# A long single-core transformer kernel: all matmuls whose result nobody reads are removed

## What is computed

```
h = x
n = rms_norm(h, ln_mix_g);  proj = n @ w_in
ya = dilated_mixture(qa, ka, va) @ w_branch_a          # softmax attention in windows, 3 dilations
yb = stick_breaking(qb, kb, vb) @ w_branch_b           # sweeps over 128-key blocks, backwards
h = h + (gate_a * ya + gate_b * yb) @ w_out
n = rms_norm(h, ln_x_g);    h = h + memory_cross_attn(n, rms_norm(mem, ln_mem_g), ...)
n = rms_norm(h, ln_ffn_g);  h = h + conv_gated_mlp(n, w_up, conv_w, conv_b, w_down)
h = rms_norm(h, ln_f_g)
# second block
p = rms_norm(h, norm_pre) @ w_in2
fox = softmax attention with a decay bias, 8 heads     # in 4 pairs of heads
mla = latent attention, 8 heads                        # in 4 pairs of heads
out = h + rms_norm([fox, mla] @ w_out2, norm_post)
```

## Time and profile before

| | |
|---|---|
| median of 3 executions | 3004.85 us (3004.74 to 3006.88) |
| profiled execution, its own time | 3007.79 us |
| its span, first to last instruction | 3006.0 us |
| TensorE busy (matmul) | 2886.6 us, 96% |
| VectorE / ScalarE / GpSimd busy | 1485.9 / 950.1 / 788.4 us |
| mean granted TensorE clock | 0.986 of full speed |

### The profile page before, as it was taken

The page is one execution under the profiler, slowest core; times in us unless marked ns, Lnnn a source line. Parts: engine busy times, 40 slices in busy tenths (PEclk is TensorE's granted clock), DMA queues, the critical chain, the costliest instruction groups (busy, mean ns, idle before and its releaser), DMA issues.

```text
span 3006.0 us, 36445 instructions
## 1 busy us (share of the span) xinstructions
PE 2886.6 (96%) x13664; PEld 2249.3 (75%) x13664; DVE 1485.9 (49%) x1765; ACT 950.1 (32%) x1536; POOL 788.4 (26%) x514
## 2 busy tenths in 40 slices
PE   6999999999999999999999999999999999999998
PEld 5888785566577777677888888887787777877766
DVE  7464565644543335444433444433426655377764
ACT  4322226655600003232221221112214444254441
POOL 5312202322233331103332233232121011231225
PEclk8999999999999999999999999999999999999999
DMA  6200100000111110101111111111201001000023
GB/s 211 71 22 29 36 15 8 22 22 19 63 46 45 48 44 28 36 15 49 49 42 49 49 49 42 49 49 42 84 23 29 22 22 26 11 7 6 15 99 119
DMA packets 166342, 128.62 MB, mean 43 GB/s; under 512 B 19264, under 2 KB 150048, under 8 KB 165968
## 3 DMA queue, kind: packets, MB, share of 16 engines
q1 hardware_dynamic: 164816, 118.55, 13.0%
q10 hardware_dynamic: 1408, 8.50, 0.7%
HBM read 114.20 MB, written 12.65 MB: 42 GB/s over the span
## 4 chain that ended last, share of the span: by engine, by line
PE 64%; DVE 6%; ACT 1%; issue 1%; DMA 1%; POOL 0%; SPq 0%; DVEq 0%; ACTq 0%; POOLq 0%
PE ps L723 17%; PE ps L725 16%; PE ps L724 16%; PE ps L2825 2%; PE ps L2665 2%; PE ps L636 2%; PE ps L2720 1%; PE ps L2921 1%; PE ps L2721 1%; PE ps L2722 1%; PE ps L2922 1%; PE ps L2923 1%; DVE max_parts L2291 1%; DVE dF L2236 1%; PE ps L2897 1%
## 5 line engine op out<-in xcount | busy, mean ns | idle before, releaser
L723 PE MATMUL ps<-NH,w_high 128*128 128x512 f32 (+2 forms) x1992 | 772.3, 388 | 14.1 <-POOL w_low L1070 8.0
L724 PE MATMUL ps<-NL,w_high 128*128 128x512 f32 (+2 forms) x1992 | 772.9, 388 | 0.0
L725 PE MATMUL ps<-NH,w_low 128*128 128x512 f32 (+2 forms) x1992 | 770.1, 387 | 0.0
L1068 POOL CAST w_high<-w_raw 128x1024 fp32r<-128x1024 f32 x193 | 208.0, 1078 | 1931.8 <-PE ps L725 1147.0
L1070 POOL TENSOR_TENSOR w_low<-w_raw,w_high 128x1024 fp32r<-128x1024 f32 x193 | 480.8, 2491 | 15.4
L723 PEld LDWEIGHTS ps<-NH,w_high 128*128 128x128 f32 x1992 | 376.8, 189 | 101.8 <-issue 11.0
L724 PEld LDWEIGHTS ps<-NL,w_high 128*128 128x128 f32 x1992 | 376.6, 189 | 77.5
L725 PEld LDWEIGHTS ps<-NH,w_low 128*128 128x128 f32 x1992 | 376.9, 189 | 76.9
L819 DVE TENSOR_TENSOR hT<-hT,ps 128x1024 f32<-128x1024 f32 x168 | 205.1, 1221 | 250.2 <-PE ps L725 250.2
L723 PE MATMUL ps<-act_high,w_high 128*128 128x512 f32 x352 | 141.3, 401 | 2.9 <-DVE act_low L1968 2.9
L725 PE MATMUL ps<-act_high,w_low 128*128 128x512 f32 x352 | 139.4, 396 | 0.0
(11 more groups left out here) (406 smaller groups left out, 5279.5 us busy)
## 6 DMA issues: line engine op xcount, KB each, us to landing
w_raw<-in_w_in SPq DMA_DIRECT2D x69, 512.0 KB, 3.8
w_raw<-in_w_up SPq DMA_DIRECT2D x44, 512.0 KB, 3.8
w_raw<-in_w_out SPq DMA_DIRECT2D x24, 512.0 KB, 3.5
w_raw<-in_w_down SPq DMA_DIRECT2D x22, 512.0 KB, 3.8
w_raw<-in_w_xkv SPq DMA_DIRECT2D x8, 512.0 KB, 5.6
x_in<-in_x SPq DMA_DIRECT2D x8, 512.0 KB, 9.1
residual_spill<-hT SPq DMA_DIRECT2D x1, 4096.0 KB, 13.6
hT<-residual_spill ACTq DMA_DIRECT2D x1, 4096.0 KB, 13.0
```

What stands on the lines that cost most here:

```text
L723: nc.tensor.matmul(o, wh, xh, start=start, stop=False)
L724: nc.tensor.matmul(o, wh, xl, start=False, stop=False)
L725: return nc.tensor.matmul(o, wl, xh, start=False, stop=stop)
L1068: nc.gpsimd.tensor_copy(WH[slot][:, :], w_raw[slot][:, :]).then_inc(w_high, 1)
```

## The change

`busy` and all its calls are taken out. Nothing else differs: no wait, buffer, order or size. The argument `rows_gap` of `attend_pe` stays and is no longer used.

```
         def norm_pe(pe, name, first=0):
...
             norm_rows(pe, name)
-            if name in UPDATED:
-                busy(bank[1], 14)
...
-        def busy(o, n):
-
-            for _ in range(n):
-                nc.tensor.matmul(o, identb, masks[:, 0:4, :].rearrange("p a b -> p (a b)"), start=True, stop=True)
...
                         b = bank[A.bank(unit)]
-                        if (h, g, u) == (0, 0, 0):
-                            busy(b, 11)
                         pe.wait_ge(a_row, 2 * p + h + 1)
...
                             products(n - 2)
-                        if n == 0:
-                            wait_bank(pe, SB, i, U + 3)
-                            busy(bank[SB.bank(U + 3)], 8)
                         if n < 24:
                             sums(n)
...
-            busy(bank[0], 28)
             pe.wait_ge(g_m, G.iters + 2)
...
-            busy(bank[0], 32)
             pe.wait_ge(f_lo, FFN.iters * 2 + 4)
...
                         wait_bank(pe, st, i, U + unit)
-                        if n == 0:
-                            busy(bank[st.bank(U + unit)], rows_gap)
                         pe.wait_ge(p_rows[h], pb * 32 + 32)
...
             wait_bank(pe, MLA, 0, 0)
-            busy(bank[MLA.bank(0)], 20)
...
                 wait_bank(pe, OUT, 0, u)
-            busy(bank[0], 6)
             for g in range(2):
```

## The result

The changed kernel takes 3038.14 us (median of 4, 3034.67 to 3040.79); the kernel before, run beside it, 3005.77 us (median of 4). The ratio is 1.0106, 95% interval 1.0092 to 1.0119: 1.1% slower, 32 us. I had forecast 3024 us with a range of 3013 to 3034. The direction was right, the size was not: the measured time lies above the range.

The account below looks back on a forecast made before the run. TensorE, busy for 96% of the span, was taken to bound the kernel. Falls of its clock at the emptied waits, 3.4 + 4.0 + 2.0 + 6.0 + 0.3 + 1.6 + 1.4 = 18.7 us, on 3004.85 gave 3024 us, range 3013 to 3034.

Parts of the forecast that it names:

- end of `G`: One wait of 7.30 us at the end of loop `G`: the clock falls, costing 2.0 us.
- `FFN`: One wait of 9.90 us at the loop's end: the clock falls already, 1.70 us are paid, so only 0.3 more.
- the norms: Three waits of 3.80 us in norms `x`, `ffn`, `fin`: nothing hides a fall, 2.0 us each, 6.0 together.
- rival 4: The extra matmuls do not hold the clock, which falls anyway; time 3005 us; chance 0.03.
- rival 3: In the norms, `G` and `A` the engine feeding TensorE is slower and covers the slow stretch; 3003.8 us; chance 0.05.
- rival 1: Short waits, the four of `SB` and four of `FOX`, cost nothing; time 3018 us; chance 0.20.
- `SB`: Four waits of 2.30 us ahead of the sweeps: eight in ten fall at 1.25 us each, 4.0 together; bounds 0 and 13.6.
- `MLA`: One wait of 5.90 us: the clock falls, VectorE covers some of it, costing 1.4 us; bounds 0 and 2.25.
- `A`: Two waits of 3.30 us: both fall, 1.70 us each, 3.4 together; bounds 0 and 2 x 2.25.
- `FOX`: Four waits of 1.50 us: three in ten fall at 1.30 us each, 1.6 together; bounds 0 and 5.2.
- `OUT`: Start of `OUT`: any gain or fall is hidden in a later 3.23 us wait for a weight tile; 0 us.
- Rival 2: The clock stays down longer behind `SB`'s waits: each of four costs 3.4 us, sum 28.3, time 3033; chance 0.17.

Follow-up runs that it names:

- experiment 3: Kernel before without the extra matmuls of the three norms and of the ends of `G` and `FFN`: 3017.06 us, 1.0037.
- experiments 4 to 6: Kernel before, extra matmuls of `SB` and `MLA` moved behind the wait: 8 of 512 columns 3026.06 us; 32 of 128, bf16, 3024.17; 16 of 128, float32r, 3035.37.
- experiment 8: Kernel before without the extra matmuls of `A` (11 in each of two passes) and `FOX` (4 in each of four pairs): 3016.60 us, 1.0023.
- experiment 10: Kernel before with none ahead of `OUT` and more extra matmuls ahead of `A`, its second pass and `SB`, in `F0` and at `FFN`'s end: 2999.45 us, 0.9973.
- experiment 2: Kernel before without the 20 extra matmuls ahead of `MLA` alone: 3012.51 us, 1.0016.
- experiments 5 and 6: Kernel before, extra matmuls of `SB` and `MLA` replaced behind the wait by 32 of 128 columns in bf16 (3024.17 us) or 16 in float32r (3035.37 us).
- experiment 7: Kernel before without the 6 extra matmuls ahead of `OUT` alone: 3005.73 us, 0.9993.

## Why the prediction was right or wrong

**Right.** What bounds the kernel, and that next to nothing but the granted clock would move: the other engines' busy times, the waits and the order are the same, the mean clock fell. That long waits ahead of dense products cost about 2 us each: end of `G` 1.3 to 2.2, `fin` 1.6, `ffn` 1.4 in one profile and 2.9 in two. That `FFN` had paid already. The sum over `G` and the norms, 8.0 forecast and 8.5 and 8.0 in two profiles, is partly luck: experiment 3 gave 10.5, and norm `x` cost 3.8 in the first profile, in place of 2.0. Of that, 2.1 us fell on the sums of squares ahead of the wait, which I had not priced; the norm also costs 0.9 to 1.5 us more in six of nine profiles of kernels that keep its extra matmuls. That the extra matmuls hold the clock (rival 4 fell), that VectorE does not cover the norms (rival 3 fell; the dense product behind norm `x` alone took 1.6 us more), and that short waits cost too: rival 1 fell, and with it the estimate that I had made by the advice of the Trainium skill, "TensorE: Matmul & The Clock Gate", section "Why this matters for your kernels": the trace does not agree with about 3 us as a bound. The four waits of 2.1 us in `SB` cost 8.1 to 11.4 us together.

**Wrong: the price behind a wait.** The step that failed is "`MLA`, one wait of 5.90 us ... so it shares the pace: 2.0 less some cover: **1.4**. Bounds 0 and 2.25", and with it the 1.25 for a fall in `SB`. I had taken the length of the low stretch from waits that dense 512-column products follow, 3.4 to 4.5 us, and carried it to places where narrow float32r matmuls follow. There it is 12 to 13 us of work in `MLA` and 6.8 to 13.7 us in the sweeps of `SB`, up to three times as long, and experiments 4 to 6 show that what ends a low stretch is the kind of work behind the wait. 8 wide or 32 narrow bf16 matmuls ended it after 3.4 us in the sweeps where the clock was down (after 5.3 us with the 8 in `MLA`), 16 narrow float32r ones of the same total length did not. Which property of the work decides is open. `MLA` measured 5.5 to 6.1 in place of 1.4, with a half-clock stretch that VectorE covers hardly at all, and `SB` 8.1 to 11.4 in place of 4.0. In the first profile these two are 10.7 of the 11.1 us by which the spans' difference of 29.8 is above my 18.7. That they make up nearly all of it is again luck: what else I missed (`A` -3.2, `FOX` +2.6, `OUT` -1.2 and some small ones) about cancels.

Rival 2 is the one that came true in `SB`: in the first profile three of four falls cost more than its 2 us. It named the mechanism, put it at 13.6 at most and at 0.17 in chance, and I did not ask the same of `MLA`, whose bound of 2.25 was too low by more than a factor of two. The row for it was there: the norm's 5.00 us at 0.50 with TensorE busy for 4.31 of them. I read it as something of tiny matmuls, and not as a sign that the busy time of the profile and what keeps the clock up are two things.

**`FOX`, mis-sized:** 1.6 forecast, 4.1 measured, 6.4 against a profile without falls of its own there. The price of a fall, 1.1 to 1.5 us, was near that of the earlier trace rows; but in place of three in ten there were five falls in four pairs, three of them at waits that I had left out because nothing was removed there (experiment 8).

**`A`, not settled by one run:** 3.4 forecast, 0.2 and 5.7 in two profiles of the same kernel, 1.9 in experiment 8. The same wait of 3.3 us made the clock fall in three of six cases. My rule that a wait above 2.9 us makes it fall rested on a few waits and was too firm.

**`OUT`, wrong in sign and small:** "the fetch ... comes at the end of a chain that does not run over TensorE". It does, through the weight slot, GpSimd and its collision with VectorE: -1.2 us, not 0. In the changed kernel most of this is lost again behind the fetch, where the clock is down for 6.8 us in place of 3.4.

## What to carry to other kernels

Price a wait of TensorE by the work behind it, not by its own length: a wait of 2.1 us ahead of narrow float32 matmuls cost up to 3.2 us here (1.7 to 3.2), one of 7.1 us ahead of dense ones 1.3 to 2.2. Matmuls into a free bank inside such a wait cost nothing when they end before the wait does, and holding the clock with them was worth 1.1% of this kernel, though they did not hold it every time (experiment 10); six of them that ended too late cost 1.2 us. A profile of the kernel before has falls of its own: take the price of a place from more than one of them. A chance that a small term is large in one place should be asked of every place with the same kind of work.

## What was not expected of the hardware

- TensorE can be recorded as busy for 12.85 of 13.00 us and stay at 1.2 GHz throughout (experiment 2), with matmuls of 128 to 400 columns, 50 of the 55 in float32r, each with a weight load of its own. The Trainium skill, "TensorE: Matmul & The Clock Gate", section "The HAM clock gate (the "warmup" mystery)", describes the throttle as following how busy TensorE has been; busy by the profile's matmul records is not enough here.
- Two sorts of matmul of the same width differ: 32 in bf16, 0.10 us apart at half clock, brought the clock back; 16 in float32r, 0.21 us apart, did not where it was down when they began (experiments 5 and 6).
- The same wait, 3.3 us in `A`, is followed by full clock in one execution and by 6.9 us at half clock in another, so single profiles of one kernel differ by up to 3 us in such a place.
- With the extra matmuls of `A` and `FOX` taken out, the clock fell at two waits of 1.43 us in `FOX` that had held none, in three profiles of three; in the ten profiles with them it never fell there (experiment 8).
- A start of GpSimd's difference of two tiles 1.2 us earlier against VectorE's products changed three products of VectorE from 3.66 + 1.96 to 2.84 + 1.56 us (experiment 7).
